# Two transformer blocks on one core: the second block's projections in three passes, weight rests on GpSimd, x parked in memory

## The chip, the cores and the metric

The kernel runs on one core of a Trainium2 chip. The metric is the device time of one execution in microseconds. Before the change the median of three runs is 1591.18 us (1590.16 to 1595.38). The profile shows one execution of its own. In it PE is TensorE, DVE is VectorE, ACT is ScalarE, POOL is GpSimd and SP is SyncE, whose queue issues most transfers.

## The reference, cut to what matters

The first block (attention with a chosen set of keys, a gated recurrence, latent attention, then a gated feed-forward part) ends in an RMS norm. The second block, on 512 tokens of width 1024 in float32, is where the change is:

```python
x = rms_norm(x, final_norm)                   # end of the first block
h = rms_norm_2(x, norm_g) * (1 + scale) + shift
proj = h @ w_in                               # 1024 -> 2840 columns
q, kcr, vcr, ksl, vsl, kwn, vwn, z_a, g_br, u, z_s = split(proj)
attn = nsa_attention(q, compress(kcr), compress(vcr), ksl, vsl, kwn, vwn, sigmoid(g_br)) * silu(z_a)
y = gelu(s5_mixer(u, ...))                    # state space recurrence
ssm = y * sigmoid(y @ glu_w + glu_b) * silu(z_s)
x = x + gate * (concatenate([attn, ssm]) @ w_out)
```

## The kernel before, in words

**Layout.** Activations lie transposed, 128 features by 512 tokens to a tile. `X` (tensor `x_sb`) and `H` (`h_sb`) hold eight such tiles each. The weights come in chunks of up to 128 x 2048 through a ring of four slots, in the order of `plan()`. SP waits for the last use of a slot (`used`) before it loads the next chunk there. Some steps of the second block stand in SP's queue among these loads: the four state space loads and the wait for the sums ahead of `rows2_s`, the 16 transfers of u (`u4_in`) ahead of `rows2_w`, the 16 transfers of y (`y_in`, L616) ahead of `cmp_k2`.

**Two ways to multiply.** Most products of the first block are made in three passes (`triple`, L690 to L700): a float32 operand is cut into a head (rounded to fp32r) and a rest, and the product is head x head + head x rest + rest x head. The heads of the weights are made by ACT in pieces of up to 1024 columns (`weight_heads`, L1348 to L1360, into one of four places of `heads`), the rests by DVE in the ring itself (`weight_rests`, L1816). PE waits for "split p" before it first uses piece p, and `heads_used` tells ACT when the place of a head is free. The second block's projections are plain float32 products instead (`product`, L685). The page records each of them as two matmuls.

**The second block's projections.** There are 34 units, each with one output bank: 14 of a 128 x 512 tile with 8 products (`proj2_0` to `proj2_6`, two units to a chunk: u, kcr, vcr, za, zs), and 20 of rows (128 tokens x 256 columns with 8 products, the four last 24 columns wide; `rows2_q0`, `q1`, `s`, `w`, `g`). ACT drains each bank (`drain`, L1328). PE's order is written by hand: 4 full units and 9 rows, then a wait for "ssm matrices" of DVE, the state space's out weights (L1099, L1100), 8 groups of transposes (L1107), and for each of four groups b of the recurrence a "bu" product (L1118), some units (`SIDE`, 5, 5, 5 and 4) and the output y of the group before (L1132 to L1134). Behind the fourth y come the 2 units that are left, then glu (L685 with `tiles`), the compression of keys and values (L1145) with turns (L822), then attention and the output product.

**DVE in that time.** After the last feed-forward tile it makes the norms' factors, two diagonals (L1728) and `scale_by_spread` (L1737, eight tiles, each followed on ACT by L1610, which adds the shift in `H`). Then it builds the state space matrices (`fold_out_weights`, `next_out_weights`, `next_in_weights`; 48 operations of 128 x 512, of L1816 but for one of L1822), sets "ssm matrices", makes two sets of phases, scales `X` by the final norm (L1822) and runs the recurrence's groups.

**POOL** does 7 small powers (L2590) and 32 comparisons in the first block's bias (L2587).

Of the kernel before, what the change touches and what calls it, by code (L numbers as in the profile page):

```python
# [7 lines left out]
F32 = mybir.dt.float32  # L8
# [7 lines left out]
P = 128  # L16
# [137 lines left out]
def plan():  # L154
# [26 lines left out]
    proj2 = [(f"proj2_{i}", len(c) * tile) for i, c in enumerate(by_twos(PROJ2))]  # L181
    out += proj2[:2] + [(f"rows2_{n}", KD * width(parts)) for n, parts in ROWS2] + proj2[2:]
# [142 lines left out]
def two_blocks_kernel(nc, wstream, ssm, xT, consts, small, pos_row, pos_col, pos_key, gated, outT, known):  # L325
# [36 lines left out]
    work_r, tiles_r = rounded("work", 4608), rounded("tiles", 22 * T)  # L362
    X = x_sb[:, :].rearrange("p (k t) -> p k t", k=KD)
# [95 lines left out]
    SIDE = [5, 5, 5, 4]  # L459
# [84 lines left out]
    y_full, y_done = sem("y_full"), sem("y_done")  # L544

# [45 lines left out]
    with block:  # L591
# [52 lines left out]
        def _(pe):  # L644
# [45 lines left out]
            def triple(out, name, c, n, ah, ar, start, stop, last=False, moving=False):  # L690
# [3 lines left out]
                if p not in split_seen:  # L694
                    split_seen.add(p)
                    pe.wait_ge(dve_step, at(f"split {p}"))
# [616 lines left out]
        def _(act):  # L1313
# [36 lines left out]
            def weight_heads(n=1, upto=None):  # L1350

                for p in range(made[0], made[0] + n if upto is None else upto):
# [4 lines left out]
                    if p >= PIECES:  # L1357
                        act.wait_ge(heads_used, p - PIECES + 1)
# [238 lines left out]
            for j in range(8):  # L1597
                if j < 7:
                    weight_heads(4)
                act.wait_ge(turn_done, at(f"added final {j}"))  # L1600
                if j >= 3:
# [5 lines left out]
            step(act.activation(ROOT2, MEAN2, ACT.Sqrt), "root block2")  # L1607
            for k in range(KD):
                act.wait_ge(dve_step, at(f"scaled block2 {k}"))
                step(act.activation(H[:, k, :], H[:, k, :], ACT.Identity, bias=MOD[:, k:k + 1]), f"normed block2 {k}")  # L1610
            scale2 = {"za": 0.5, "zs": 0.25}
            dest2 = {"kcr": 0, "vcr": 1, "u": 2, "za": 6, "zs": 10}
            def drains2():
                def project2(tiles_):
                    for n, i in tiles_:
# [1014 lines left out]
```

## Time and profile before

| what | value |
| --- | --- |
| median of three runs | 1591.18 us (1590.16 to 1595.38) |
| the profiled execution | 1588.68 us, its span 1586.8 us |
| PE busy | 1432.6 us, 90% of the span |
| DVE busy | 950.3 us, 60% |
| ACT busy | 511.9 us, 32% |
| POOL busy | 52.7 us, 3% |
| PE's share of the chain that ended last | 54% (the rest of it is in smaller pieces) |
| mean granted clock of PE | 0.949 |

The second block begins at about 1129 us of the span, where PE has ended the last feed-forward product. Its projections run until 1348 us, glu until 1362 us, compression until 1398 us, attention until about 1530 us, and the output product to the end. A matmul's recorded length overlaps the next, so its true pace is read from the distance of two starts, or from a merged row of the chain.

### The profile page before, as it was taken

What the parts mean: (1) busy time and instruction counts of PE and PEld (TensorE: products, weight loads), DVE (VectorE), ACT (ScalarE), POOL (GpSimd) and SP (SyncE); (2) the same over time, 40 slices, a digit from 0 to 9 for tenths busy, and PEclk for the clock granted to TensorE, in tenths of its full rate; (3) what the DMA queues carried; (4) which work ended last, traced back from release to release, by engine and by line L of the source; (5) the groups of instructions that cost most, each with busy time, mean ns of one, the idle gap of its engine ahead of it and who ended that gap; (6) DMA issues with size and microseconds to landing.
All of it is one profiled execution on the core that took longest, in us unless ns stands there. A gap on an engine that the chain in (4) does not pass through costs nothing.

```text
span 1586.8 us, 18674 instructions
## 1 busy us (share of the span) xinstructions
PE 1432.6 (90%) x7046; PEld 1092.9 (69%) x7046; DVE 950.3 (60%) x1601; ACT 511.9 (32%) x824; POOL 52.7 (3%) x43
## 2 busy tenths in 40 slices
PE   5998888896989877999899999999798999988998
PEld 4758788785567655787688888888567954566653
DVE  6259767676166768774545545533493748868730
ACT  5346332331322554233323423423313221223310
POOL 0000000000000450000000000000000002000000
PEclk9999999997989979999899999999898999989999
DMA  5212111121222120353134443222421122520001
GB/s 223 75 53 81 67 41 54 61 90 49 84 107 80 47 74 27 136 209 107 53 136 156 186 159 143 73 77 106 133 82 37 58 76 80 186 80 1 1 1 53
DMA packets 39881, 140.49 MB, mean 89 GB/s; under 512 B 13041, under 2 KB 17521, under 8 KB 27249
## 3 DMA queue, kind: packets, MB, share of 16 engines
q1 hardware_dynamic: 34608, 130.53, 23.4%
q10 hardware_dynamic: 5184, 8.78, 1.5%
q8 instruction: 56, 0.92, 0.2%
q14 instruction: 33, 0.26, 0.0%
HBM read 128.42 MB, written 8.39 MB: 86 GB/s over the span
## 4 chain that ended last, share of the span: by engine, by line
PE 54%; DVE 4%; ACT 1%; issue 1%; ACTq 0%; DVEq 0%
PE turn L700 22%; PE score L685 7%; PE score L700 5%; PE sum L685 4%; PE turn L685 3%; PE sum L700 2%; PE sum L1263 2%; PE sum L1145 1%; PE score L1145 1%; PE score L1237 1%; PE turn L1249 1%; PE turn L822 1%; DVE stat L2541 1%; PE turn L1118 1%; DVE probs L1774 0%
## 5 line engine op out<-in xcount | busy, mean ns | idle before, releaser
L1816 DVE TENSOR_TENSOR ring_r<-ring,heads_r 128x1024 fp32r<-128x1024 f32 (+3 forms) x153 | 176.3, 1153 | 222.6 <-ACT heads_r L1359 187.2
L1359 ACT ACTIVATE heads_r<-ring 128x1024 fp32r<-128x1024 f32 (+3 forms) x153 | 153.4, 1002 | 241.0 <-DMA ring<-wstream 129.2
L700 PE MATMUL score<-h_sb_r,heads_r 128*128 128x512 f32 x376 | 151.6, 403 | 0.0
L700 PE MATMUL turn<-tiles_r,heads_r 128*128 128x512 f32 x336 | 132.2, 393 | 0.0
L700 PE MATMUL turn<-h_sb_r,heads_r 128*128 128x512 f32 x304 | 119.7, 394 | 8.1 <-DVE ring_r L1816 8.1
L700 PE MATMUL turn<-wide_r,heads_r 128*128 128x512 f32 x312 | 121.9, 391 | 0.0
L700 PE MATMUL turn<-wide_r,ring_r 128*128 128x512 f32 x312 | 121.6, 390 | 0.0
L700 PE MATMUL score<-x_sb_r,heads_r 128*128 128x512 f32 x256 | 110.1, 430 | 8.9 <-DVE ring_r L1816 6.5
L700 PE MATMUL score<-x_sb_r,ring_r 128*128 128x512 f32 x256 | 103.8, 405 | 0.0
L700 PEld LDWEIGHTS score<-h_sb_r,heads_r 128*128 128x128 f32 x376 | 73.9, 197 | 13.9 <-issue 0.2
L700 PEld LDWEIGHTS turn<-tiles_r,heads_r 128*128 128x128 f32 x336 | 64.1, 191 | 13.3
L700 PEld LDWEIGHTS turn<-h_sb_r,heads_r 128*128 128x128 f32 x304 | 57.9, 190 | 20.5 <-issue 8.3
L700 PE MATMUL sum<-h_sb_r,heads_r 128*128 128x512 f32 x168 | 67.7, 403 | 0.0
L700 PEld LDWEIGHTS score<-x_sb_r,heads_r 128*128 128x128 f32 x256 | 51.2, 200 | 23.6 <-issue 10.6
L700 PEld LDWEIGHTS turn<-wide_r,heads_r 128*128 128x128 f32 x312 | 58.9, 189 | 12.4
L700 PEld LDWEIGHTS turn<-wide_r,ring_r 128*128 128x128 f32 x312 | 58.8, 188 | 12.2
L700 PEld LDWEIGHTS score<-x_sb_r,ring_r 128*128 128x128 f32 x256 | 50.8, 198 | 11.5
L1682 ACT ACTIVATE tiles<-score,stat 128x128 f32<-128x128 f32 (+3 forms) x64 | 33.7, 527 | 74.2 <-issue 62.2
L685 PE MATMUL score<-h_sb,ring 128*128 128x512 f32 x128 | 55.8, 592 | 0.0
L2590 POOL TENSOR_TENSOR stat<-stat,cst 128x4 f32<-128x4 f32 (+4 forms) x7 | 16.1, 2295 | 1180.8 <-DVE stat L1819 803.9
L1328 ACT ACTIVATE tiles<-score 128x512 f32<-128x512 f32 x39 | 24.3, 622 | 93.4 <-PE score L685 41.9
L700 PE MATMUL turn<-h_sb_r,ring_r 128*128 128x512 f32 x128 | 50.5, 395 | 0.0
(399 smaller groups left out, 2952.5 us busy)
## 6 DMA issues: line engine op xcount, KB each, us to landing
ring<-wstream SPq DMA_DIRECT2D x95, 1024.0 KB, 4.9
ring<-wstream SPq DMA_DIRECT2D x16, 704.0 KB, 4.4
ring<-gated SPq DMA_DIRECT2D x6, 1024.0 KB, 6.9
gated<-tiles ACTq DMA_DIRECT2D x15, 256.0 KB, 2.0
gated<-probs ACTq DMA_DIRECT2D x9, 256.0 KB, 2.0
x_sb<-xT SPq DMA_DIRECT2D x4, 512.0 KB, 5.7
x_sb<-xT ACTq DMA_DIRECT2D x1, 2048.0 KB, 8.3
outT<-x_sb SPq DMA_DIRECT2D x1, 2048.0 KB, 6.3
```

What stands on the lines that cost most here:

```text
L685: mm = pe.matmul(out, l, r, start=(i == 0), stop=(i == len(pairs) - 1))
L700: return pe.matmul(out, a, w, **k) if moving else pe.matmul(out, w, a, **k)
L822: mm = pe.transpose(b[0:src.shape[1], dst:dst + r], src, ident[0:r, 0:r])
L1118: mm = pe.matmul(b[:, jj * P:(jj + 1) * P], BT[z][:, j, :], U4[:, j, :], start=True, stop=True)
L1145: mm = pe.matmul(b[0:2 * NCMP, 0:256], CB[kv][:, 8 * i + l, :], w[:, l, :], start=(i + l == 0), stop=(8 * i + l == 31))
L1237: pe.matmul(PAIR_OF(p)[:, e * T:e * T + cols], TL[r, 18 + j, n * P:(n + 1) * P], KT2[r, 2 * a_ + j // 2, 0:cols], start=True, stop=False)
L1263: mm = pe.matmul(OUT[g][:, h % 4 * P:h % 4 * P + P], PROBT(i)[:, j * P:(j + 1) * P], R2[:, j, at_v:at_v + P], start=(j == 0), stop=(j == n))
L1328: step(act.activation(out, b, func, bias=bias, scale=scale), name, gemm_done)
L1359: step(act.activation(head_piece(p), chunk(name)[:, c:c + cols], ACT.Identity), f"head {p}")
L1682: step(act.activation(PROB(i)[:, 0:cols], PAIR_OF(p)[:, i % 2 * T:i % 2 * T + cols], ACT.Exp, bias=stat[:, 8 + i % 4:9 + i % 4], scale=1.0 ...
L1816: step(dve.tensor_tensor(out, a, b, op), name)
L2590: step(pool.tensor_tensor(v, v, half.broadcast_to([P, n]), ALU.pow), f"rstd {name}")
```

## The change

The 34 units of the second block's projections are made in three passes. What that takes:

- The input's head goes to `X`'s place (`X_HEAD`, by ACT), its rest to `H` (`H_REST`, by eight new operations of DVE, one behind each scaled tile). `X` itself is written to memory before (eight transfers of 256 KB on ACT's queue, one for each finished tile, into `gated`) and loaded again after the last unit (one of 2 MB on ACT's queue).
- The projections' weights become 23 pieces (22 of 1024 columns, one of 192). ACT makes their heads, in six places that are free then (the constants `level`, `chosen`, and `tiles` 6 to 13), by a fixed table `HOME2` and right behind certain drains (`heads_through`). POOL makes the rests. PE waits for POOL's semaphore.
- The first two units run side by side (`split_pair`). 14 units follow ahead of the state space's matrices (12 of rows among them, 9 before). `SIDE` is 5, 5, 4 and 4, and no unit is left behind the fourth y.
- The scaling of `X` by the final norm leaves DVE. POOL does it in 16 operations, behind its last power, and DVE waits for it before the first `wout2` addition.

```diff
+    PLACES2 = [cst_r[:, coff["level"][0]:coff["level"][0] + PIECE], chosen_r[:, :]] + \
+              [tiles_r[:, (6 + 2 * z) * T:(8 + 2 * z) * T] for z in range(4)]
+    HOME2 = [0, 1, 2, 3, 4, 5, 0, 1, 2, 3, 4, 5, 2, 0, 1, 4, 5, 4, 5, 0, 1, 0, 1]
+    def home_free(q):
+        earlier = [i for i in range(q) if HOME2[i] == HOME2[q]]
+        return earlier[-1] + 1 if earlier else 0
+    def heads_through(q):
+        n = q + 1
+        while n < len(HOME2) and n <= q + 4 and home_free(n) <= q + 1:
+            n += 1
+        return FIRST2 + n
...
-    SIDE = [5, 5, 5, 4]
+    SIDE = [5, 5, 4, 4]
...
-                    pe.wait_ge(dve_step, at(f"split {p}"))
+                    pe.wait_ge(pool_step if p >= FIRST2 else dve_step, at(f"split {p}"))
...
-            first = feature_units("proj2", PROJ2, lambda k: H[:, k, :], ready=(act_step, [f"normed block2 {k}" for k in range(KD)]))
-            units = itertools.chain(*[row_units(f"rows2_{n}", width(parts), H) for n, parts in ROWS2], first)
-            run(first, 4)
-            run(units, 9)
+            acts2 = [(X_HEAD[:, k, :], H_REST[:, k, :]) for k in range(KD)]
+            outs = [gemm_bank()]
+            up(gemm_full)
+            outs.append(gemm_bank())
+            for mm in split_pair(outs, [("proj2_0", 0), ("proj2_0", KD * P)], acts2, [f"split block2 {k}" for k in range(KD)]):
+                mm.then_inc(gemm_full, 1)
+            up(gemm_full, "used proj2_0")
...
+            units = itertools.chain(whole_units(1, 2), *[split_rows(f"rows2_{n}", width(parts), acts2) for n, parts in ROWS2], whole_units(2, 7))
+            run(units, 14)
...
                 act.wait_ge(turn_done, at(f"added final {j}"))
+                act.dma_start(gated[j], X[:, j, :]).then_inc(parked, 16)
...
+            weight_heads(2)
+            act.wait_ge(parked, 16 * KD)
             for k in range(KD):
                 act.wait_ge(dve_step, at(f"scaled block2 {k}"))
-                step(act.activation(H[:, k, :], H[:, k, :], ACT.Identity, bias=MOD[:, k:k + 1]), f"normed block2 {k}")
+                step(act.activation(X_HEAD[:, k, :], H[:, k, :], ACT.Identity, bias=MOD[:, k:k + 1]), f"head block2 {k}")
...
+            act.dma_start(X, gated[0:KD].rearrange("b p t -> p b t")).then_inc(x_again, 16)
...
-            scale_by_spread("block2", lambda k: GAIN2[:, k:k + 1], H, "scaled")
+            def rest_of_block2(k):
+                dve.wait_ge(act_step, at(f"head block2 {k}"))
+                stt(H_REST[:, k, :], H[:, k, :], MOD[:, k:k + 1], X_HEAD[:, k, :].bitcast(F32), ALU.add, ALU.subtract, f"split block2 {k}")
+            scale_by_spread("block2", lambda k: GAIN2[:, k:k + 1], H, "scaled", lambda k: k and rest_of_block2(k - 1))
+            rest_of_block2(KD - 1)
...
-            for k in range(KD):
-                stt(X[:, k, :], X[:, k, :], sm("g_final")[:, k:k + 1], rstd_final, ALU.mult, ALU.mult)
...
+            dve.wait_ge(pool_step, at("x scaled"))
...
+                    for p in range(FIRST2, len(pieces)):
+                        of, c, cols = pieces[p]
+                        pool.wait_ge(act_step, at(f"head {p}"))
+                        step(pool.tensor_tensor(chunk(of, ring_r)[:, c:c + cols], chunk(of)[:, c:c + cols], head_piece(p).bitcast(F32), ALU.subtract),
+                             f"split {p}")
...
+            pool.wait_ge(x_again, 16)
+            for k in range(KD):
+                step(pool.tensor_scalar(X[:, k, :], X[:, k, :], sm("g_final")[:, k:k + 1], None, ALU.mult))
+                step(pool.tensor_tensor(X[:, k, :], X[:, k, :], rstd_final, ALU.mult), "x scaled" if k == KD - 1 else None)
```

The order of PE's work from the fourth y (the L1132 to L1134 rows, then in the change L1170 to L1172) to the compression, before and then with the change:

```order
L1132 MATMUL sum<-tiles,toep 128x128
L1133 MATMUL sum<-work,rows 128x127
L1134 MATMUL sum<-work,heads 128x127
L685 MATMUL score<-h_sb,ring 128x512 x8
L685 MATMUL sum<-h_sb,ring 128x512 x8
L685 MATMUL score<-tiles,ring 128x512 x8
L685 MATMUL sum<-tiles,ring 128x512 x4
```

```order
L1170 MATMUL sum<-tiles,toep 128x128
L1171 MATMUL sum<-work,rows 128x127
L1172 MATMUL sum<-work,heads 128x127
L709 MATMUL score<-tiles,ring 128x512 x8
L709 MATMUL sum<-tiles,ring 128x512 x4
```

The two units with `h_sb` (za or zs tiles) that stood between the last y and glu (`tiles,ring`) are ahead of the last y now.

The order of POOL from the last comparison to its last power but one, before and with the change (`cst_r`, `chosen_r` and `tiles_r` are the places of the heads):

```order
L2587 TENSOR_SCALAR work<-prow,wide 128x128 x8
L2590 TENSOR_TENSOR stat<-stat,cst 128x32
L2590 TENSOR_TENSOR stat<-stat,cst 128x8 x2
```

```order
L2644 TENSOR_SCALAR work<-prow,wide 128x128 x8
L2649 TENSOR_TENSOR ring_r<-ring,cst_r 128x1024
L2649 TENSOR_TENSOR ring_r<-ring,chosen_r 128x1024
L2649 TENSOR_TENSOR ring_r<-ring,tiles_r 128x1024 x4
L2649 TENSOR_TENSOR ring_r<-ring,cst_r 128x1024
L2649 TENSOR_TENSOR ring_r<-ring,chosen_r 128x1024
L2649 TENSOR_TENSOR ring_r<-ring,tiles_r 128x1024 x4
L2649 TENSOR_TENSOR ring_r<-ring,tiles_r 128x192
```

POOL has 23 subtractions now where it had none (12 of the 1024-column ones and the short one are shown).

The order of DVE at the hand-over, before (first) and with the change, where each scaled tile but the first is followed by a rest:

```order
L1728 TENSOR_TENSOR work<-cst,stat 128x512 x2
L1737 SCALAR_TENSOR_TENSOR h_sb<-x_sb,stat,turn 128x512 x8
L1740 MEMSET stat 128x1
L1774 COPY wide<-turn 128x512
```

```order
L1779 TENSOR_TENSOR work<-cst,stat 128x512 x2
L1788 SCALAR_TENSOR_TENSOR h_sb<-x_sb,stat,turn 128x512 x2
L1873 SCALAR_TENSOR_TENSOR h_sb_r<-h_sb,stat,x_sb_r 128x512
L1788 SCALAR_TENSOR_TENSOR h_sb<-x_sb,stat,turn 128x512
L1873 SCALAR_TENSOR_TENSOR h_sb_r<-h_sb,stat,x_sb_r 128x512
```

Eight operations of DVE stand newly between the scaled tiles and the state space matrices.

## Rows read from the trace of the kernel before

**Rows 1.** The chain that ended last, in time: start us, us, instructions (x records):
```profile
1144.36 7.10 PE sum L685 x16
...
1199.69 3.45 PE sum L685 x16
...
1299.68 13.73 PE score L685 x32
```

**Rows 2.** Timeline of PE: start us, us, engine, line, operation, x instructions:
```profile
133.78 0.28 PE L700 MATMUL score<-heads_r,x_sb_r 128*128 128x256 f32 x1
...
134.38 0.28 PE L700 MATMUL score<-ring_r,x_sb_r 128*128 128x256 f32 x1
...
1122.01 0.39 PE L700 MATMUL turn<-h_sb_r,heads_r 128*128 128x512 f32 x1
...
1128.58 0.39 PE L700 MATMUL turn<-work_r,ring_r 128*128 128x512 f32 x1
...
1254.42 1.94 PE L685 MATMUL sum<-ring,h_sb 128*128 128x24 f32 x16
```

**Rows 3.** Timeline of DVE, the hand-over to the second block and after:
```profile
1139.65 1.42 DVE L1728 TENSOR_TENSOR work<-cst,stat 128x512 f32<-128x512 f32 x2
1142.65 6.23 DVE L1737 SCALAR_TENSOR_TENSOR h_sb<-x_sb,stat,turn 128x512 f32<-128x512 f32 x8 [1.59 <-PE turn L805]
1149.04 0.69 DVE L1774 COPY wide<-turn 128x512 f32<-128x512 f32 x1
...
1186.87 0.69 DVE L1816 TENSOR_TENSOR heads<-cst,sml 128x512 f32<-128x512 f32 x1
...
1195.26 6.26 DVE L1822 SCALAR_TENSOR_TENSOR x_sb<-x_sb,sml,wide 128x512 f32<-128x512 f32 x8
1227.12 0.69 DVE L1816 TENSOR_TENSOR heads<-turn,work 128x512 f32<-128x512 f32 x1 [25.61 <-PE turn L1118]
```

**Rows 4.** Timeline of DVE ahead of the last attention; brackets: idle before:
```profile
1370.01 1.42 DVE L1774 COPY rows<-turn 128x512 f32<-128x512 f32 x2 [2.26 <-PE turn L822]
...
1374.63 1.42 DVE L1774 COPY rows<-turn 128x512 f32<-128x512 f32 x2 [0.45 <-PE turn L822]
...
1393.11 1.42 DVE L1774 COPY tiles<-turn 128x512 f32<-128x512 f32 x2 [0.96 <-PE turn L822]
```

**Rows 5.** Timelines of PE, ACT and SP from the last y to glu:
```profile
1348.37 7.03 PE L685 MATMUL score<-tiles,ring 128*128 128x512 f32 x16
...
1334.89 0.60 ACT L1640 ACTIVATE tiles<-sum 128x512 f32<-128x512 f32 x1 [3.09 <-PE sum L1134]
...
1335.52 10.26 SPq L616 DMA_DIRECT2D tiles<-tiles  x16
```

**Rows 6.** DMA issues: line, queue, xcount, KB each, median us to landing:
```profile
tiles<-tiles SPq DMA_DIRECT2D x16, 64.0 KB, 2.0
```

**Rows 7.** Timeline of POOL and DVE where both work (the bias steps):
```profile
553.02 1.25 POOL L2587 TENSOR_SCALAR work<-prow,wide 128x384 f32<-128x384 f32 x1
553.04 0.77 DVE L1819 TENSOR_SCALAR work<-prow,wide 128x384 f32<-128x384 f32 x1
...
560.78 0.42 DVE L1819 TENSOR_SCALAR work<-prow,wide 128x384 f32<-128x384 f32 x1
...
572.27 1.22 DVE L1816 TENSOR_TENSOR ring_r<-ring,heads_r 128x1024 fp32r<-128x1024 f32 x1
572.29 1.98 POOL L2587 TENSOR_SCALAR work<-prow,wide 128x256 f32<-128x256 f32 x1
```

**Rows 8.** Groups of POOL by form: xcount | busy us, mean ns | idle before:
```profile
L2587 POOL TENSOR_SCALAR work<-prow,wide 128x512 f32<-128x512 f32 x8 | 12.8, 1601 | 155.8 <-PE score L840 142.8 <-PE score L1011 12.4
```

**Rows 9.** Timeline of ACT, a weight head, then around the hand-over:
```profile
256.14 1.06 ACT L1359 ACTIVATE heads_r<-ring 128x1024 fp32r<-128x1024 f32 x1
...
1138.14 0.20 ACT L1607 ACTIVATE stat<-stat 128x4 f32<-128x4 f32 x1 [1.99 <-DVE stat L1819]
```

**Rows 10.** Busy time by window: us, each engine's busy (x), clock, DMA share, GB/s:
```profile
1128.00:1144.00 16.00, 7.15 (x25) 4.26 (x23) 8.64 (x24) 4.08 (x8) 0.00 (x0) 0.68 0.75 196
```

More of the change, by code:

```diff
@@ L180, in plan @@
     out += [(f"down_{j}_{z}", [6 * P, 5 * P]) for j in range(8) for z in range(2)]
-    proj2 = [(f"proj2_{i}", len(c) * tile) for i, c in enumerate(by_twos(PROJ2))]
-    out += proj2[:2] + [(f"rows2_{n}", KD * width(parts)) for n, parts in ROWS2] + proj2[2:]
+    proj2 = [(f"proj2_{i}", [tile] * len(c)) for i, c in enumerate(by_twos(PROJ2))]
+    out += proj2[:2] + [(f"rows2_{n}", [KD * 24] if n == "g" else [tile, tile]) for n, _ in ROWS2] + proj2[2:]
     out += [("glu", 4 * 512)]
@@ L362, in two_blocks_kernel @@
     work_r, tiles_r = rounded("work", 4608), rounded("tiles", 22 * T)
+    cst_r, chosen_r = rounded("cst", sum(CONST.values())), rounded("chosen", PIECE)
     X = x_sb[:, :].rearrange("p (k t) -> p k t", k=KD)
@@ L1086, in _, with whole_units @@
             spread("final", 1)
-            first = feature_units("proj2", PROJ2, lambda k: H[:, k, :], ready=(act_step, [f"normed block2 {k}" for k in range(KD)]))
-            units = itertools.chain(*[row_units(f"rows2_{n}", width(parts), H) for n, parts in ROWS2], first)
-            run(first, 4)
-            run(units, 9)
+            acts2 = [(X_HEAD[:, k, :], H_REST[:, k, :]) for k in range(KD)]
[5 more added lines that the diff above has]
+            up(gemm_full, "used proj2_0")
+            def whole_units(first, last):
+                for i in range(first, last):
+                    for e in range(2):
+                        split_product(gemm_bank()[:, :], f"proj2_{i}", e * KD * P, acts2).then_inc(gemm_full, 1)
+                        up(gemm_full, f"used proj2_{i}" if e else None)
+                        yield
+            units = itertools.chain(whole_units(1, 2), *[split_rows(f"rows2_{n}", width(parts), acts2) for n, parts in ROWS2], whole_units(2, 7))
+            run(units, 14)
             pe.wait_ge(dve_step, at("ssm matrices"))
@@ L1356, in weight_heads @@
                         act.wait_ge(slot_in[i % SLOTS], 16 * (i // SLOTS + 1))
-                    if p >= PIECES:
+                    if p >= FIRST2:
+                        if home_free(p - FIRST2):
+                            act.wait_ge(heads_used, FIRST2 + home_free(p - FIRST2))
+                    elif p >= PIECES:
                         act.wait_ge(heads_used, p - PIECES + 1)
@@ L1640, in gelu @@
                 step(act.activation(TL[:, 2 + b, :], O[0][:, :], ACT.Gelu_apprx_tanh), f"y gelu {b}", y_done)
-            for _ in range(13):
+            for _ in range(16):
                 next(units)
```

14 lines of the change are left out of this document (13 added, 1 removed).

## Prediction

> **What bounds the kernel now.** I read the chain that ended last first. From 1144 us on it runs almost without a break through PE's plain float32 units: a full unit (16 records) is 13.73 / 2 = 6.87 us, a unit of rows 3.45 us, and the first stretch ends at 1199.69 + 3.45 = 1203.1 us [rows 1]. The timeline of PE gives the pace of three-pass products elsewhere in this trace: 29 starts from 1122.01 to 1128.58 are 0.2265 us apart at 512 columns, 5 starts are 0.12 us apart at 256 columns [rows 2]. Eight tiles by three passes are 24 matmuls, so 5.44 us a full unit and 2.88 us a unit of rows. The short units (24 columns) don't profit: their 16 records take 1.78 us, 0.11 us each, far more than 24 columns need, so 24 of them cost 2.66 us.
>
> The timeline of DVE says what stands behind PE. It is idle for 25.6 us before its first recurrence operation at 1227 us, and the matrices that PE waits for at 1203.1 were complete at 1187.6 us [rows 3]. So PE bounds this stage and DVE has 15.5 us of slack. Later this turns: ahead of the last attention DVE runs nearly back to back, and waits for PE five times only, 2.26 us and then four times 0.45 to 0.96 us, 5.5 us together [rows 4].
>
> **The parts of the change.** The sum is made against the profiled execution, 1588.7 us; the median of the three runs lies 2.5 us above it. A measurement of this kernel can tell about 0.3%, 4.8 us, from no change.
>
> *PE's work.* 14 full units save 14 x 1.43 = 20.0 us, 16 of rows 16 x 0.57 = 9.1, the 4 short ones cost 4 x 0.88 = 3.5. That is 25.6 us of PE time. The rest is about how little of it arrives.
>
> *The start.* The parking issues on ACT stand ahead of the squares; only the last is on the path. An issue is 10.26 / 16 = 0.64 us on SP [rows 5]; I take 0.5 on ACT. The landing (2.0 us for small ones [rows 6], more at 256 KB) is hidden: ACT writes over X only 14 us later. The scaled tiles began at 1142.65 and each took 0.78; now each is followed by a rest of about 0.75, so 16 operations of 0.77 take 12.3 us where PE needs only 1.36 us for each pair of tiles. The pair is paced by DVE.
>
> *The lock between DVE and POOL, which is the largest term.* POOL now reads two operands of 1024 columns 23 times while DVE does operations with two SBUF operands. What that costs DVE the trace shows only in small [rows 7]. A comparison of DVE that starts 0.02 us behind one of POOL takes 0.77 us in place of 0.42: DVE stood for 0.35 us of POOL's 1.25, with 384 columns and one operand. The other way round POOL's operation of 256 columns, started 0.02 us behind a subtraction of DVE, takes 1.98 us, more than the 1.60 it takes for twice the columns [rows 8]: it stood for most of DVE's 1.22. So the two exclude each other while they read. Scaled by what is read (2 x 1024 against 384), one rest of POOL costs DVE 0.35 x 5.33 = 1.9 us. The bounds: nothing (DVE slips in between), and 3.2 us (DVE stands for the whole operation, taken as twice the 1.60 us of 512 columns [rows 8]). I take 1.9, since that row is of the same two engines. The Trainium skill, SBUF — State Buffer, "Who interferes with whom", says that the port pair goes to whichever starts first for the whole instruction, and that a DVE instruction with two SBUF inputs contends with a GpSimd one that reads SBUF. By that rule DVE would have stood for all 1.25 us in that row; it stood for 0.35, so the trace agrees with the exclusion and not with its length. With the whole operation the sum comes out as in rival B, 1608, with the row as here, 1592.6.
>
> *Step by step with 1.9 us.* ACT's root of the block 2 norm ends at 1138.34 [rows 9]; behind it now come two weight heads of 1.06 [rows 9]. The first one's rest starts on POOL at about 1139.9, just ahead of DVE's diagonals (1139.65 + 0.5 [rows 3]), and holds them 1.7 us. The scaled tiles start at 1142.65 + 0.5 + 1.7 = 1144.85, the last rest is done at 1157.2, the pair at 1158.6. Before, the same two units ended at 1144.36 + 13.7 = 1158.1. The new passes gain nothing here.
> Then 2 full units and 12 of rows: 1158.6 + 10.9 + 34.6 = 1204.1 us, when PE wants the matrices. (Before it was 1203.1 with three units of rows less.) DVE's 48 operations, the copy before them and the clearing behind took 1149.04 to 1187.6, 38.5 us [rows 3]. From 1157.2 they would end at 1195.7, with 8 us of slack. But pieces 4 to 11 and 13 get their heads between 1159 and 1206, so 9 rests of POOL fall in here: 9 x 1.9 = 17.1, and DVE is done at 1212.8. PE stands for 8.7 us, and goes on 9.7 us later than before.
> To the end of the fourth bu product (1299.5) there were 7 units of rows, 4 short, 4 full (58.8 us), and there are 4, 4 and 6 now (54.7): -4.1, so +5.6. Four full units before the last y's: -5.7, so -0.1 at the fourth y.
>
> *The transfers of y.* The last gelu ended at 1335.5, SP then issued 16 transfers in 10.26 us [rows 5], which land 2.0 us after [rows 6], so at 1347.8, and glu started at 1348.37 [rows 5]. The two units that stood there hid all of it. Without them PE waits for 0.9 + 10.3 + 2.0 = 13.1 us, and I add 1.5 us for a low clock as glu begins: in the 16 us of the hand-over, PE mostly idle, the granted clock was 0.68 on the mean, some 10 us of it at 1.2 GHz [rows 10]. 14.6 against 13.7: +0.9, so glu at +0.8. The change takes 10.9 us of work out of this gap and puts it ahead of it; that work isn't hidden any more by anything.
>
> *DVE ahead of the attention.* Its chain starts with the fourth bu product at +5.6. Two late rests (pieces 21 and 22) fall in it, +3.8. It gets back what it waited for PE, -5.5 [rows 4]. That is +3.9, later than PE's +0.8, so the attention starts at +3.9.
>
> *At nothing.* X's scaling leaves DVE (6.26 us [rows 3]), but DVE was idle behind it; the cover is 25.6 us. On POOL it takes 16 operations of 512 columns, some 16 x 1.6 = 26 us [rows 8], from about 1405 to 1430, 100 us before the output product asks for it. If DVE waits for a few of these reads in the attention, up to +3; not below nothing. ACT's 23 heads (23 x 1.06) lie in the gaps between its drains (some 3 to 6 us each). The 2 MB load runs beside y's transfers; these are limited by their issue.
>
> **Sum:** +3.9 us, 1592.6; with the small unknowns I say **1593 us**, within 0.3% of before.
>
> **Rivals.** *A: DVE hardly waits for POOL.* For it: POOL's reading was over within 0.4 us of 1.25 in the row, and a later DVE operation might slip in. With no cost: pair done at 1156.9, PE at the matrices at 1202.4 and DVE ready at 1194; -0.7, then -4.8 at the fourth bu, -10.5 at the fourth y, -9.6 at glu, DVE -10.3. Sum -9.6: 1579. It decides below about 1.2 us a rest (there -4.5).
> *B: POOL holds DVE for nearly its whole operation.* With 3.2 us: DVE's matrices at 1158.5 + 38.5 + 28.8 = 1225.8, so +22.7, at the fourth bu +18.6, DVE's chain + 6.4 - 5.5 = +19.5: 1608. It decides from about 2.0 us on, close above what I took, and is thus nearly as likely. For it: two operands on one engine may be read slower than one. The GPSIMD Engine Reference of the Trainium skill, section 3.1, has a subtraction's sibling, an add of 2048 columns, at 4497 ns, by which one of 1024 would be an estimated 2.25 us; if all of that held DVE, the sum would be 12 us more for each us, +8, 1597. No row here shows such an operation.
> *C: rests come too late for PE.* Pieces 17, 18, 21 and 22 get their head only after the drain of the unit before the one ahead of them: 5.44 us for drain 0.6, head 1.06 and rest. It costs nothing up to 3.8 us a rest, and 4 us for each us above. Against it: 3.2 us is the upper bound.
> *D: the change's passes aren't faster.* No: 1.43 us a unit is read at the same clock and shape.
>
> **How the numbers follow.** Forecast (1.2 to 2.0 us a rest; -4.5 to +4.8, 1584 to 1593.5) 0.36; A 0.34; B with C 0.30. The last two reach 1579 and 1608; of B's range I leave the far end out: **1577 to 1604**. Faster by over 0.3%: 0.34, within 0.36, slower 0.30.
>
> **What would show it.** Full units of 24 records at 5.44 us, rows at 2.88. A gap of PE ahead of the L1137 products (before L1099), 8.7 us by the forecast, none by A, 20 by B, with DVE's operations of 0.69 us stretched to 2.5 wherever POOL works. An idle PE of some 13 us between the fourth y and glu. DVE's waits ahead of the attention gone. If rests of POOL overlap unstretched operations of DVE, the lock is wrong; if the gap before glu is missing, the reading of y's transfers is; if PE waits for POOL between full units, C.

## The result and the profile after

The median goes from 1591.05 us (1590.16 to 1595.38, four runs) to **1607.18 us** (1606.51 to 1608.88, four runs): 1.010 times the time before, with an interval from 1.0077 to 1.0124. The forecast was 1593, within 0.3% of before; the range ended at 1604. The kernel is 16 us slower, and outside the range. The profiled execution took 1606.51 us, its span is 1604.7 us, 17.9 us longer than before.

PE has less to do, and everybody else more: PE is busy for 1423.4 us (1432.6 before), DVE for 991.7 (950.3), ACT for 536.1 (511.9), POOL for 133.2 (52.7). In the new kernel the names of before stand at other lines: passes L724 (L700), plain products L709 (L685), the state space's first products L1137 (L1099), its transposes L1145 (L1107), DVE's tensor_tensor L1867 (L1816), POOL's rests L2649.

The timeline of DVE from the hand-over on (start us, us, engine, line, operation, shapes, x instructions, idle before in brackets) answers to [rows 3]:

```profile
1140.03 5.57 DVE L1779 TENSOR_TENSOR work<-cst,stat 128x512 f32<-128x512 f32 x2
...
1164.24 0.69 DVE L1867 TENSOR_TENSOR heads<-heads,stat 128x512 f32<-128x512 f32 x1
1164.97 2.78 DVE L1867 TENSOR_TENSOR rows<-rows,heads 128x512 f32<-128x512 f32 x1
1167.78 2.78 DVE L1867 TENSOR_TENSOR rows<-heads,stat 128x512 f32<-128x512 f32 x1
1170.60 2.76 DVE L1867 TENSOR_TENSOR heads<-rows,stat 128x512 f32<-128x512 f32 x1
1173.39 0.69 DVE L1867 TENSOR_TENSOR heads<-rows,heads 128x512 f32<-128x512 f32 x1
...
1213.42 1.76 DVE L2370 MEMSET toep<- 128x2048 f32 x1 [0.49 <-DVE tiles L1867]
1215.22 0.69 DVE L1867 TENSOR_TENSOR heads<-cst,sml 128x512 f32<-128x512 f32 x1
```

The timeline of POOL in the same stretch, with its first rest ahead of it:

```profile
1120.54 2.40 POOL L2649 TENSOR_TENSOR ring_r<-ring,cst_r 128x1024 fp32r<-128x1024 f32 x1 [530.01 <-ACT cst_r L1400]
...
1139.96 5.09 POOL L2649 TENSOR_TENSOR ring_r<-ring,tiles_r 128x1024 fp32r<-128x1024 f32 x2 [14.55 <-ACT tiles_r L1400]
1164.25 5.77 POOL L2649 TENSOR_TENSOR ring_r<-ring,tiles_r 128x1024 fp32r<-128x1024 f32 x2 [19.20 <-ACT tiles_r L1400]
1170.41 2.41 POOL L2649 TENSOR_TENSOR ring_r<-ring,cst_r 128x1024 fp32r<-128x1024 f32 x1 [0.39 <-ACT cst_r L1400]
...
1186.64 5.49 POOL L2649 TENSOR_TENSOR ring_r<-ring,tiles_r 128x1024 fp32r<-128x1024 f32 x2 [8.11 <-ACT tiles_r L1400]
```

Read the two together. POOL starts a rest at 1164.25, just behind a DVE operation that runs to the end undisturbed (1164.24, 0.69 us). The next DVE operation takes 2.78 us in place of 0.69, and so on as long as POOL goes on: DVE loses 2.09 us to each rest, of the 2.40 us that a rest takes where DVE is idle beside it (1120.54). Nine full rests and a small one fall in the matrices. At the diagonals (1140.03) two fall in: 5.57 us in place of 1.42. The matrices, complete at 1187.6 before [rows 3], are complete at 1215.9, in the operation that starts at 1215.22.

PE, its timeline (a wait of its own in brackets):

```profile
1148.33 0.77 PE L724 MATMUL sum<-x_sb_r,cst_r 128*128 128x512 f32 x1 [0.54 <-DVE h_sb_r L1873]
```

```profile
1215.97 0.63 PE L1137 MATMUL score<-rows,tiles 128*32 128x128 f32 x2 [8.20 <-DVE heads L1867]
...
1229.31 0.86 PE L1145 MATMUL score<-cst,tiles 128*128 128x128 f32 x4 [2.07 <-ACT tiles L1366]
...
1236.00 1.97 PE L1145 MATMUL score<-cst,tiles 128*128 128x128 f32 x8 [1.59 <-ACT tiles L1366]
```

```profile
1340.27 0.49 PE L1170 MATMUL sum<-tiles,toep 128*128 128x128 f32 x2 [2.02 <-ACT tiles L1690]
...
1358.68 9.12 PE L709 MATMUL score<-tiles,ring 128*128 128x512 f32 x16 [15.47 <-issue]
```

PE stands for 8.2 us ahead of the L1137 products, which start at 1215.97 (1203.1 before). Behind them the transposes end 14.5 us later than before (1236.00 against 1221.47 for the same group), since PE's first products behind the stall run at 1.2 GHz (the row at 1215.97 has 0.63 us where the same takes 0.38 to 0.41 at 2.4 GHz). Ahead of glu it stands for 15.5 us.

The windows of 10 us (busy of each engine with counts, granted clock, DMA share, GB/s), first before, then after:

```profile
1250.00:1260.00 10.00, 10.00 (x65) 9.66 (x64) 9.42 (x18) 0.95 (x4) 0.00 (x0) 0.83 0.31 105
1260.00:1270.00 10.00, 10.00 (x60) 8.73 (x60) 2.58 (x5) 5.33 (x7) 0.00 (x0) 0.83 0.14 36
```

```profile
1250.00:1260.00 10.00, 10.00 (x91) 10.00 (x90) 9.69 (x10) 3.15 (x6) 4.78 (x2) 1.00 0.32 105
1260.00:1270.00 10.00, 10.00 (x48) 9.90 (x48) 9.42 (x18) 0.78 (x4) 0.00 (x0) 0.52 0.01 2
1270.00:1280.00 10.00, 10.00 (x37) 7.93 (x37) 9.59 (x12) 1.27 (x2) 2.60 (x1) 0.80 0.30 105
```

A window at 1.2 GHz throughout would show 0.50. Before, 0.83 and 0.83 make 6.8 us at 1.2 GHz; after, 0.52 and 0.80 make 13.6 us. In both kernels the clock falls while the short units (24 columns) run, 2.2 us behind the first short record before (at 1256.6) and 7.8 us behind it after (at 1260.3). PE had then been busy without a gap for over 20 us.

DVE from the third bu product to the attention:

```profile
1317.03 0.69 DVE L1867 TENSOR_TENSOR heads<-turn,work 128x512 f32<-128x512 f32 x1 [5.70 <-ACT work L1686]
...
1321.38 5.65 DVE L2406 TENSOR_TENSOR_SCAN heads<-stat,heads 128x128 f32<-128x128 f32 x8
1327.07 2.87 DVE L1867 TENSOR_TENSOR work<-heads,work 128x512 f32<-128x512 f32 x1
1329.97 0.69 DVE L1867 TENSOR_TENSOR rows<-heads,work 128x512 f32<-128x512 f32 x1
...
1344.80 6.13 DVE L1867 TENSOR_TENSOR wide<-wide,stat 128x512 f32<-128x512 f32 x9 [2.83 <-POOL stat L2652]
...
1403.24 1.42 DVE L1825 COPY tiles<-turn 128x512 f32<-128x512 f32 x2 [1.25 <-PE turn L846]
...
1407.86 1.42 DVE L1825 COPY tiles<-turn 128x512 f32<-128x512 f32 x2 [0.97 <-PE turn L846]
...
1413.28 0.42 DVE L2597 TENSOR_REDUCE stat<-score 128x2 f32<-128x256 f32 x1 [1.47 <-PE score L1278]
```

The fourth bu product reaches DVE at 1317.03 (1303.31 before). Two rests of POOL lengthen the scans from 3.64 to 5.65 us and an operation from 0.69 to 2.87. At 1344.80, ahead of the nine operations, DVE is 17.9 us late (1326.89 before). Two waits for PE are left of five [rows 4], and the attention's first reduction comes at 1413.28, 14.7 us late (1398.54 before). At the end of the span it is 17.9 us again.

So the way of the 17.9 us is: +3.8 at the end of the first pair of units (PE drained it at 1161.9, before 1158.1), +12.9 at L1137, +14.5 at the transposes, +13.7 at the fourth bu product, +17.9 on DVE ahead of its squares, +14.7 at the attention, +17.9 at the end.

### The profile page after: what moved, and what is told of

The parts are those of the page before. It is cut to its first block, busy times and chain, and to the rows that moved or that the text cites. A ratio compares the mean times of both kernels' runs of the same rounds, so it can differ in the third digit from the quotient of the medians.

```text
span 1604.7 us, 19347 instructions
## 1 busy us (share of the span) xinstructions
PE 1423.4 (89%) x7317; PEld 1124.7 (70%) x7318; DVE 991.7 (62%) x1601; ACT 536.1 (33%) x847; POOL 133.2 (8%) x82
## 4 chain that ended last, share of the span: by engine, by line
PE 45%; DVE 14%; issue 1%; ACT 1%; POOL 0%; ACTq 0%; DVEq 0%; POOLq 0%
PE turn L724 22%; PE score L724 8%; PE sum L724 4%; PE turn L709 3%; DVE heads L1867 2%; PE sum L1301 2%; DVE rows L1867 2%; DVE work L1867 1%; DVE wide L1867 1%; PE score L1275 1%; PE sum L1183 1%; DVE tiles L1867 1%; PE turn L1287 1%; DVE stat L2597 1%; DVE probs L1825 1%
## 5 line engine op out<-in xcount | busy, mean ns | idle before, releaser
L1867 DVE TENSOR_TENSOR ring_r<-ring,heads_r 128x1024 fp32r<-128x1024 f32 (+3 forms) x153 | 176.3, 1152 | 222.1 <-ACT heads_r L1400 186.6
L724 PE MATMUL score<-h_sb_r,heads_r 128*128 128x512 f32 x376 | 151.7, 403 | 0.0
L724 PE MATMUL turn<-tiles_r,heads_r 128*128 128x512 f32 x336 | 132.1, 393 | 0.0
L724 PE MATMUL score<-x_sb_r,ring_r 128*128 128x512 f32 x320 | 129.7, 405 | 0.0
L724 PE MATMUL turn<-h_sb_r,heads_r 128*128 128x512 f32 x304 | 119.7, 394 | 8.1 <-DVE ring_r L1867 8.1
L724 PE MATMUL turn<-wide_r,heads_r 128*128 128x512 f32 x312 | 121.9, 391 | 0.0
L724 PE MATMUL turn<-wide_r,ring_r 128*128 128x512 f32 x312 | 121.6, 390 | 0.0
L724 PE MATMUL score<-x_sb_r,heads_r 128*128 128x512 f32 x256 | 110.4, 431 | 8.9 <-DVE ring_r L1867 6.5
L724 PEld LDWEIGHTS score<-h_sb_r,heads_r 128*128 128x128 f32 x376 | 74.0, 197 | 14.0 <-issue 0.2
L724 PEld LDWEIGHTS turn<-tiles_r,heads_r 128*128 128x128 f32 x336 | 64.1, 191 | 13.4
L724 PEld LDWEIGHTS score<-x_sb_r,ring_r 128*128 128x128 f32 x320 | 63.2, 197 | 14.3
L724 PEld LDWEIGHTS turn<-h_sb_r,heads_r 128*128 128x128 f32 x304 | 57.8, 190 | 20.5 <-issue 8.3
L724 PE MATMUL score<-ring_r,x_sb_r 128*128 128x256 f32 (+3 forms) x240 | 68.3, 285 | 0.0
L724 PEld LDWEIGHTS score<-x_sb_r,heads_r 128*128 128x128 f32 x256 | 51.4, 201 | 23.4 <-issue 10.4
L724 PE MATMUL sum<-h_sb_r,heads_r 128*128 128x512 f32 x168 | 67.8, 403 | 0.0
L724 PEld LDWEIGHTS turn<-wide_r,heads_r 128*128 128x128 f32 x312 | 58.8, 189 | 12.2
L724 PEld LDWEIGHTS turn<-wide_r,ring_r 128*128 128x128 f32 x312 | 58.8, 189 | 12.2
L724 PE MATMUL sum<-x_sb_r,ring_r 128*128 128x512 f32 x160 | 65.7, 411 | 0.0
L2649 POOL TENSOR_TENSOR ring_r<-ring,cst_r 128x1024 fp32r<-128x1024 f32 x5 | 12.3, 2458 | 544.3 <-ACT cst_r L1400 544.2
```

What stands on the lines that cost most here:

```text
L724: return pe.matmul(out, a, w, **k) if moving else pe.matmul(out, w, a, **k)
L1867: step(dve.tensor_tensor(out, a, b, op), name)
```

## Experiments

Each time is a median of four or more executions, and each ratio is to executions of the kernel before that were timed beside them. The same code runs ahead of the changed part in all of them, and yet its end moves: where no rest meets the first diagonal, PE's L829 products start between 1139.4 and 1142.7 us from one profile to the next. So times of two kernels that differ by less than some 3 us are not told apart by one profile.

**1. No rests on POOL.** The subtraction is left out: ACT writes a copy of the weights.

```diff
-                        step(pool.tensor_tensor(chunk(of, ring_r)[:, c:c + cols], chunk(of)[:, c:c + cols], head_piece(p)..., ALU.subtract),
-                             f"split {p}")
...
+                        step(act.activation(chunk(name, ring_r)[:, c:c + cols], chunk(name)[:, c:c + cols], ACT.Identity), f"split {p}")
```

> Leaves out the subtraction of the second block's weight rests: ACT writes a copy of the weights in their place (1.06 us a piece more on ACT), POOL has no rests. Theory (POOL's rests hold DVE, 2.09 us each, in the matrices and in the last recurrence): no DVE operation of 128x512 above 0.8 us between 1139 and 1330; the matrices are done near 1193 in place of 1216, PE's gap of 8.2 us ahead of the L1137 products is gone, and these start 12 us earlier; DVE's 4.2 us ahead of the squares go too. 1607 - 12 - 4 = 1591, up to 3 more if DVE then waits for PE. Rival (the loss is PE's: low clock and the 15.5 us idle ahead of glu, the stretched DVE operations are mostly covered): at most 5 us, 1602.

Measured: 1586.33 us, ratio 0.9995 (0.9979 to 1.0011). DVE and PE of this kernel:

```profile
1191.04 1.76 DVE L2372 MEMSET toep<- 128x2048 f32 x1 [0.49 <-DVE tiles L1869]
```

```profile
1202.26 0.28 PE L724 MATMUL sum<-ring_r,x_sb_r 128*128 128x256 f32 x1
1202.46 0.41 PE L1137 MATMUL score<-rows,tiles 128*32 128x128 f32 x2
```

The matrices' last clearing is at 1191.04 in place of 1213.42, no operation is stretched, PE goes from its rows to L1137 without a gap, 13.5 us earlier, and the fourth bu product reaches DVE at 1302.22. POOL's rests cost the change some 17 us by the two ratios (1.010 and 0.9995), 21.6 us between the two profiles. But without them it only draws level with before, where rival A had said 1579. The low clock of the short units is there too (0.79 and 0.52 in 1240 to 1260, 13.8 us at 1.2 GHz), so it comes without the stall and without the rests. The other losses have to be found elsewhere.

**2. One unit less ahead of the fourth bu product; 3. two units behind the fourth y.**

```diff
-    SIDE = [5, 5, 4, 4]
+    SIDE = [5, 5, 3, 4]      (experiment 2)
+    SIDE = [5, 5, 4, 2]      (experiment 3)
```

> One full unit is moved from ahead of the fourth bu product to behind the fourth y. Theory (from the fourth bu product on DVE's chain sets the time, +13.7 us there becomes the end's +17.9): the product comes 5.4 us earlier, so does everything behind it: 1602. Rival (PE's own sum of work and clock sets it, DVE's chain has room): PE's order changes but not its work, only what fills the 15.5 us idle ahead of glu counts, also 5.4 us, but then the run with two units moved from behind the fourth bu product gains 8. The two runs together tell them apart.

> Two full units are moved from between the fourth bu product and the fourth y to behind the fourth y, as in the kernel before; what stands ahead of the fourth bu product stays. Theory (DVE's chain sets the time): the idle PE ahead of glu shrinks from 15.5 us to about 4, glu starts 6 to 8 us earlier, and the whole time stays within 2 us of 1607, because DVE starts the heads and the compressed keys no earlier. Rival (the missing cover over y's transfers is what costs): 6 to 8 us less, 1600.

Measured: 1605.25 us (ratio 1.0098, 1.0080 to 1.0117) and 1606.56 us (1.0113, 1.0098 to 1.0128). Experiment 3, PE:

```profile
1334.07 0.77 PE L1170 MATMUL sum<-tiles,toep 128*128 128x128 f32 x2 [6.40 <-DVE work L1867]
...
1352.93 7.47 PE L709 MATMUL score<-tiles,ring 128*128 128x512 f32 x13 [2.47 <-issue]
```

```profile
1373.82 8.52 PE L1183 MATMUL score<-ring,heads 128*62 128x256 f32 x32 [5.27 <-issue]
...
1397.80 1.38 PE L846 MATMUL turn<-cst,wide 128*128 128x128 f32 x8 [1.56 <-DVE tiles L1825]
```

glu starts 5.8 us earlier than in the changed kernel and the idle ahead of it is 2.5 us, but PE then waits for 5.3 us ahead of the compression and for DVE's tiles at the same place as before (1397.80). The time stays: DVE's chain sets it, and covering y's transfers alone is worth nothing. Experiment 2 brings the fourth bu product to DVE at 1312.82 and DVE's squares 6.3 us earlier, and of that only 1.35 us reach the attention: PE's glu starts no earlier (1359.49), and DVE waits 4.1 us for PE at its first turn. Of the 5.4 us expected at most 2 came, and by the ratios (1.0098 against 1.010) none that can be told from noise. The theory was wrong by the second path, PE's through y's transfers, which lies close behind DVE's.

**4. X's scaling left out, and 5. X loaded back later.** Experiment 4 scales only 8 columns of each tile on POOL; experiment 5 moves one line on ACT from ahead of glu to ahead of the attention.

```diff
+                step(pool.tensor_scalar(X[:, k, 0:8], X[:, k, 0:8], ...))            (4)
...
-            act.dma_start(X, gated[0:KD].rearrange("b p t -> p b t")).then_inc(x_again, 16)
...
+            act.dma_start(X, gated[0:KD].rearrange("b p t -> p b t")).then_inc(x_again, 16)   (5)
             for i, (a_, n, h) in enumerate(ITEMS):
```

> Leaves out X's scaling except for 8 columns of each tile. Theory (GpSimd's 16 operations of 128x512 in the attention cost the 3.2 us by which the attention took longer than before, 14.7 us late at its start and 17.9 at its end): 1604, granted clock of 1420 to 1440 up from 0.55 to some 0.8. Rival (the low clock there comes from how PE's work is broken up, DVE's reductions and copies out of PSUM aren't held by POOL): within 1 us of 1607, the same low clock.

> Only X's 2 MB are loaded back later, ahead of the attention in place of beside y's transfers. Theory (the load holds up y's transfers: glu starts 3.7 us behind the last of their issues, without it 2): PE's idle ahead of glu 13.5 us in place of 15.5, glu 2 us earlier, but the time stays within 1.5 us of 1607, since DVE's chain sets the attention's start. Rival (y's transfers are limited by their issue, the load beside them costs nothing): the idle stays 15.5 us.

Measured: 1605.38 us (1.0110, 1.0084 to 1.0135) and 1608.97 us (1.0098, 1.0068 to 1.0128). Neither can be told from the changed kernel. The granted clock of 1420 to 1440 stayed at 0.58 in experiment 4 (0.55 in the changed kernel), so the rival holds: the scaling doesn't cost the 3.2 us. From the attention's first transposes to the end of the span the changed kernel takes 189.0 us, experiment 4 188.2, the kernel before 185.9, and the others between 184.5 (experiment 1) and 191.7 (experiment 11), all with the same attention. Laid side by side with the granted clock of the first 60 us from those transposes, the lengths go with the clock:

| kernel | us to the end | clock, first 60 us |
| --- | --- | --- |
| experiment 1 | 184.5 | 0.91 |
| before | 185.9 | 0.89 |
| experiments 5 and 10 (A) | 186.2, 186.3 | 0.86 |
| experiment 12 (C) | 187.3 | 0.83 |
| experiments 4 and 6 | 188.2, 188.3 | 0.80 |
| changed, experiments 3 and 8 | 189.0 | 0.77 |
| experiments 2 and 7 | 190.4, 190.3 | 0.80 |
| experiment 11 (B) | 191.7 | 0.74 |

That is 13.2 us at 1.2 GHz before and 27.6 with the change. It is a comparison of kernels, not a test; experiments 2 and 7 lie off the line. Experiment 5's PE:

```profile
1341.46 0.49 PE L1170 MATMUL sum<-tiles,toep 128*128 128x128 f32 x2 [2.02 <-ACT tiles L1690]
...
1356.87 5.43 PE L709 MATMUL score<-tiles,ring 128*128 128x512 f32 x8 [12.47 <-issue]
```

SP's 16 issues of y end at 1355.4 there and glu starts 1.5 us later. In the changed kernel it starts 3.75 us behind them (1354.93), in experiment 2, where the load of X is issued 6 us behind the first y transfer, 7.5 us. The 2 MB load does hold up y's transfers: glu starts 2.3 us later behind the last issue, and the 16 issues themselves take 11.0 us beside it and 10.3 without it. Together that is the 3.0 us by which PE's idle time differs (15.47 and 12.47).

**6. Rests with one operand.** The subtraction is left out; POOL copies the weights.

```diff
-                        step(pool.tensor_tensor(chunk(of, ring_r)[:, c:c + cols], chunk(of)[:, c:c + cols], head_piece(p)..., ALU.subtract),
+                        step(pool.tensor_copy(chunk(of, ring_r)[:, c:c + cols], chunk(of)[:, c:c + cols]),
```

> Leaves out the subtraction: POOL writes a copy of the weights in place of the rest, so it reads one operand of 1024 columns, not two. Theory (DVE stands for as long as POOL reads, and two operands are read one after the other): POOL's operation takes about half of 2.40 us, a DVE operation that meets it about 1.7 us in place of 2.78; PE's gap of 8.2 us goes and the L1137 products start some 9 us earlier: 1596. Rival (the hold goes with POOL's columns, whatever it reads): 2.4 and 2.78 us as before, 1607.

Measured: 1592.04 us (1.001, 0.9999 to 1.0022). POOL, then DVE:

```profile
1165.18 1.48 POOL L2649 CAST ring_r<-ring 128x1024 fp32r<-128x1024 f32 x1 [0.69 <-ACT tiles_r L1400]
...
1208.54 1.05 POOL L2649 CAST ring_r<-ring 128x1024 fp32r<-128x1024 f32 x1 [0.39 <-ACT cst_r L1400]
```

```profile
1165.07 0.69 DVE L1867 TENSOR_TENSOR rows<-rows,heads 128x512 f32<-128x512 f32 x1
1165.80 1.41 DVE L1867 TENSOR_TENSOR rows<-heads,stat 128x512 f32<-128x512 f32 x1
1167.24 0.69 DVE L1867 TENSOR_TENSOR heads<-rows,stat 128x512 f32<-128x512 f32 x1
```

The copy takes 1.05 us where it doesn't stand for DVE (1208.54), and the DVE operation that meets one 1.41 us: it loses 0.72 us. POOL holds DVE for its own duration less some 0.3 us, 0.72 of 1.05 here, 2.09 of 2.40 with two operands.

**7. Short units in one pass; 8. short units between rows.** Experiment 7 leaves out two of three passes of the short units but for the last tile; experiment 8 only changes the order, on PE and in ACT's drains.

```diff
+                if name == "rows2_g" and not stop:
+                    return one(wh, ah, start=start, stop=False)          (7)
...
-            units = itertools.chain(whole_units(1, 2), *[split_rows(...) for n, parts in ROWS2], whole_units(2, 7))
+            units = itertools.chain(whole_units(1, 2), *rows2[:3], in_turns(*rows2[3:]), whole_units(2, 7))   (8)
```

> Leaves out two of three passes of the four short units (24 columns), but for their last tile: 10 records a unit in place of 24, 56 fewer, 6.2 us at 0.111 us each. Theory (the clock of 1.2 GHz between 1260 and 1273.7 comes from the 96 short records ahead of it, and gave back 6.9 of the us that the passes save): the clock stays at 2.4 GHz there, the fourth bu product comes 13 us earlier, 1594. Rival (the clock falls there whatever the short units do, from what stands ahead of them): 6 us at the fourth bu product, 1601.

> Only the order is changed: the four short units (24 columns) go one by one between the last four units of 256 columns, in place of one after the other. Theory (the fall to 1.2 GHz comes from the short records standing together): the 13.7 us at 1.2 GHz ahead of the third and fourth bu products shrink or go, the fourth product comes up to 6.9 us earlier, up to 1600. Rival (as many short records in the same 25 us pull the clock down wherever they stand): the same low stretch, 1607.

Measured: 1595.41 us (1.0024, 1.0006 to 1.0042) and 1605.86 us (1.0085, 1.0057 to 1.0113). Experiment 7's windows, to be laid beside those above:

```profile
1250.00:1260.00 10.00, 10.00 (x79) 9.51 (x79) 9.73 (x9) 4.32 (x8) 5.78 (x3) 1.00 0.42 138
1260.00:1270.00 10.00, 10.00 (x51) 8.36 (x50) 9.51 (x15) 1.20 (x2) 1.41 (x1) 1.00 0.24 83
1270.00:1280.00 10.00, 10.00 (x60) 8.79 (x59) 9.50 (x15) 6.34 (x8) 0.00 (x0) 1.00 0.24 96
```

The clock stays at 2.4 GHz, and the fourth bu product reaches DVE at 1303.11, 13.9 us earlier (1.6 of that were there at L1137 already). 6.2 us are the records left out, and what remains, 6.1 us, is the clock: 13.6 us at 1.2 GHz do the work of 6.8. Experiment 8 has 0.84, 0.79, 0.83 and 0.83 in the four windows, 14.2 us at 1.2 GHz against 13.6 in the changed kernel, and no change of the time that can be told from noise: with the short records within 17 us (1252.5 to 1269) or spread over 25 (1244.8 to 1270), as many microseconds run at 1.2 GHz.

**9. Rests on DVE.** POOL keeps the first two; the others stand in DVE's order at places that I chose from the trace: one behind the diagonals, one behind the pair, six between the matrices, the rest between and in the recurrence's groups.

```diff
+            BEHIND = {6: 1, 9: 1, 13: 1, 18: 1, 32: 1, 34: 1}
...
+                    step(dve.tensor_tensor(chunk(of, ring_r)[:, c:c + cols], chunk(of)[:, c:c + cols], head_piece(p)..., ALU.subtract),
+                         f"split {p}")
```

> The rests of pieces 2 to 22 are made by DVE (1.22 us each), POOL keeps the first two. Theory (DVE loses less by the operation than by standing for POOL's): six rests in the matrices cost 7.5 us in place of 19; matrices done at 1202 in place of 1216, PE's gap at most 1 us, fourth bu product near 1303 in place of 1317: 1589, as in the run without any rests plus 2 for two rests in DVE's last chain. Rival (DVE's order makes rests late, PE waits for them between its units): gaps of 1 to 3 us ahead of full units, 1595 or more.

Measured: 1618.48 us (1.0185, 1.0157 to 1.0213), slower than the change. PE:

```profile
1313.74 0.77 PE L724 MATMUL sum<-x_sb_r,cst_r 128*128 128x512 f32 x1 [13.02 <-DVE ring_r L1875]
...
1342.87 0.76 PE L724 MATMUL sum<-x_sb_r,chosen_r 128*128 128x512 f32 x1 [8.01 <-DVE ring_r L1875]
```

The rival holds, and more so: the matrices came as forecast (PE has no gap at L1137), but piece 19 stands behind the scans of the fourth group in DVE's order, and these wait for the fourth bu product; PE stood 13.0 us for it, and 8.0 us for piece 22. A rest on DVE is cheap, and in the wrong place it stops PE.

**10. Rests on DVE, units moved, X later; 11. with pieces 19 to 22 earlier; 12. with short units between rows.**

```diff
-    SIDE = [5, 5, 4, 4]
+    SIDE = [5, 5, 2, 4]                                     (A, B and C)
-                rests2({0: 2, 1: 1, 2: 1, 3: 1}[b])
+                rests2({0: 2, 1: 1, 2: 2, 3: 0}[b])          (B and C)
+            units = itertools.chain(..., in_turns(*rows2[3:]), whole_units(2, 7))   (C)
```

> Rests on DVE, two full units moved from ahead of the fourth bu product to behind the fourth y, X loaded back only ahead of the attention. Theory (two paths are nearly equal, DVE's from the fourth bu product and PE's through y's transfers; both are shortened here by 10.9 us): fourth bu product at 1292, PE's idle ahead of glu under 4 us, the attention starts at 1404 or earlier in place of 1415.7: 1577, faster than before by 12. Rival (rests on DVE now come in the way of its recurrences just where PE waits for pieces 17 to 22): PE gaps of 2 to 5 us ahead of the full units behind the fourth bu product, 1585.

> As the run with rests on DVE, units moved and X later, with pieces 19 to 22 earlier in DVE's order. PE's waits of 3.4 and 4.4 us for these rests go. Theory (DVE's chain behind the fourth bu product sets the time there, PE's waits were half covered): 1 to 2.5 us less, 1578. Rival (PE's path was the longer one): 5 to 8 us less, 1573.

> As the run above, and the short units one by one between the units of 256 columns. Theory (the low clock delays the third and fourth bu products, which start DVE's chain): up to 6.9 us less than the run above, 1572. Rival (the clock falls all the same): as the run above, 1578.

Measured: 1579.96 us (A, ratio 0.9937, 0.9922 to 0.9952), 1582.96 us (B, 0.9943, 0.9918 to 0.9967) and **1575.58 us** (C, 0.9901, 0.9867 to 0.9935). All three beat both kernels. A holds the edits of experiments 9 and 5 beside the one shown; B and C also move the last rest up by one place in DVE's order. C's PE:

```profile
1312.10 0.49 PE L1178 MATMUL sum<-tiles,toep 128*128 128x128 f32 x2 [2.02 <-ACT tiles L1698]
...
1328.84 6.67 PE L709 MATMUL score<-tiles,ring 128*128 128x512 f32 x15 [2.63 <-issue]
```

No wait for a rest is left, the idle ahead of glu is 2.6 us in place of 15.5, and the fourth bu product reaches DVE at 1290.36, 26.7 us earlier than in the changed kernel. What the last two edits add is not settled. B took PE's waits for pieces away (3.4 and 4.4 us in A) and wasn't faster; its nine executions lie between 1570.7 and 1587.0 us. Of the 9.4 us between the profiles of B and C, 3.3 lie ahead of the changed part and 4.4 in the attention; 1.6 lie between, which may be the clock.

## Why the prediction was wrong, point by point

- **PE's work** was right: a full unit takes 5.44 us (the chain has 10.88 us for two), a unit of rows 2.88, a short one 2.66.
- **The start** was forecast at +0.5 us at the end of the pair; it was +3.8. I let one rest meet the diagonals; both did, since POOL went from one to the next while DVE stood: 4.15 us, not 1.7. And in 1140 to 1160 the granted clock was 0.64, after PE had stood 7.1 us for the diagonals: the pair was paced by PE at 1.2 GHz, not by DVE. Its 3.3 us more didn't reach L1137, where PE waited for DVE.
- **The lock** had the right engines, number of rests (nine) and nearly the right size: 1.9 us forecast from [rows 7], 2.09 measured. Put into the forecast's own sum for eleven rests, that adds 2.1 us, 1594.7 in place of 1592.6: the size of the hold alone doesn't explain the miss. That 1.9 came so close is in part luck: the same scaling gives 0.93 us for the copy of experiment 6, which held DVE for 0.72. PE's stall was forecast at 8.7 us and was 8.2, the matrices at 1212.8 and were done at 1215.9. Of these 3.1 us, 1.2 are the start's (DVE's last scaled rest ended at 1158.4, not 1157.2), 1.7 the nine rests at 2.09, 0.3 the small one.
- **The work up to the fourth bu product** is the step that failed most: I took −4.1 us for it, all at 2.4 GHz. It gave −0.8 after the transposes, and 1.6 us had been lost ahead of them, 4.9 in all. I had counted the short units' longer records, but not the clock that goes with them and with the stall: both stretches were priced at full clock, and the rows at 2.4 GHz say nothing of it. Experiment 7 shows the first of these alone.
- **From there to y**: −5.7 forecast, −5.3 measured (8.4 at the last y). y to glu: +0.9 forecast, +1.9 measured to its start, and its first 16 records took 9.1 us in place of 7.0 at the low clock, where the forecast had 1.5. PE stood 15.5 us, not 13.1: 3.0 us are the load of X (12.5 without it, experiment 5). I was wrong to hide it behind the issues, though by experiment 5 it didn't matter here.
- **DVE's last chain**: +3.8 for two rests forecast, 4.2 measured. The waits for PE gave back 3.2 us, not 5.5, since PE was late as well: two of five stayed.
- **The attention** got 3.2 us longer, which I had at nothing. It is not POOL's scaling (experiment 4). Over the profiles its length goes with the granted clock of its first 60 us (the table of experiment 4; 0.89 before, 0.77 with the change), so the clock is the likely cause, but no run isolates it, and what sets the clock there stays open.

3.9 forecast + 3.2 (start and size of the hold, at L1137) + 4.9 (clock up to the fourth bu product) + 0.4 (the two late rests) + 2.3 (waits that stayed) + 3.2 (attention) = 17.9. So the steps that failed are these: the work of PE up to the fourth bu product was priced at 2.4 GHz throughout (−4.1 forecast, +0.8 measured), the waits of DVE for PE were to give back 5.5 us and gave back 3.2, and the attention stood at nothing (3.2 measured, cause open).

Rival B had 1608 and the time was 1607, but by other numbers: it needed 3.2 us a rest, +22.7 at L1137 and +18.6 at the fourth bu product; 2.09, +12.9 and +13.7 were measured. The 2.09 us lie just above the 2.0 from which B was to decide, but by B's own sum they give 1595 and not 1608, so its time came out by luck. Rival A's 1579 was wrong even for a kernel without any rests on POOL: that took 1586.3: its fourth bu product came 1.1 us earlier than before, where A had 4.8, with 13.8 us at 1.2 GHz ahead of it. Rival C didn't come: PE waits for no piece.

The Trainium skill, SBUF — State Buffer, "Who interferes with whom", says that the pair goes to whichever starts first for the whole instruction. I had weighed a row with 0.35 of 1.25 us against it. With the operation that this change adds, the measured hold is 2.09 of 2.40 us, so here the page is nearer than my reading, though my number came close.

## What to carry to other kernels

Work moved to an idle engine isn't free when it makes the busy one stand. A rest on GpSimd cost VectorE 2.09 us where VectorE makes it itself in 1.22; ask for the price on the engine that waits, in the operation's own shape. When shorter PE work is forecast, ask in each stretch who is next, and at what clock PE will then run: small matmuls in three passes and a stall both cost clock, here 4.9 us up to the fourth bu product. Where two paths are nearly equal, here VectorE's from the fourth bu product and TensorE's through y's transfers, an edit on one shows nothing that can be told from noise (experiments 2, 3 and 5); experiments 10 to 12, which shorten both, are faster than before.

## What the runs showed of the hardware

- POOL's hold on DVE goes with POOL's time: 2.09 of 2.40 us (two operands of 1024 columns), 0.72 of 1.05 (one operand). DVE takes one operation between two of POOL's, so back-to-back rests hit back-to-back operations (1164.97 and 1167.78, 2.78 us each).
- A DVE operation with a single SBUF operand is held too: a rounding of the phases (L1870) took 2.58 us in place of 0.43, the time of the same form where no rest meets it, as these two rows of the changed kernel show. The Trainium skill, SBUF — State Buffer, "Who interferes with whom", lists this form among those that can take the shared pair in a faster mode; the rows agree.

```profile
1254.47 2.58 DVE L1870 TENSOR_SCALAR heads<-rows 128x512 f32<-128x512 f32 x1
...
1261.29 0.43 DVE L1870 TENSOR_SCALAR work<-rows 128x512 f32<-128x512 f32 x1
```

- Operations of DVE that read PSUM beside SBUF weren't met by a rest in the changed kernel's trace. In the attention they ran undisturbed beside POOL's scaling: this one, from `score` in PSUM and a constant in SBUF, beside a TENSOR_SCALAR of POOL from 1434.43 to 1435.99, took 1.23 us as in the kernel before, and so did the copies out of PSUM (0.62 us for two at 1427.88, as before).

```profile
1434.78 1.23 DVE L1867 TENSOR_TENSOR heads<-score,cst 128x1024 f32<-128x1024 f32 x1 [6.29 <-PE score L1237]
```

- With 96 records of 24 columns PE's granted clock was 1.2 GHz for 13.6 us, though PE was busy without a gap; with 40 of them it stayed at 2.4 GHz (experiment 7). The kernel before has 64 and 6.8 us.
- A load of 2 MB beside 16 transfers of 64 KB made PE's wait for them 3.0 us longer: 0.7 in their issues, 2.3 behind the last.
